# Seven half-size products instead of eight for the retention half of the merge, with the sums of tokens and weights on GpSimd

## The reference

```
y_mla = mla_branch(...) * silu(gate_mla)                 # 1024 x 1024
y_ret = retention_branch(q, k, v) * silu(gate_ret)       # 1024 x 2048, with a gain g_ret per column
merged = (sigmoid(merge_mla) * (y_mla @ w_proj_mla)      # weight 1024 x 1024
          + sigmoid(merge_ret) * (y_ret @ w_proj_ret))   # weight 2048 x 1024
x = x + gate * (merged @ w_out);  out = rmsnorm(x, g_final)
```

## Time and profile before

| | |
|---|---|
| runs | 1599.46, 1597.55, 1598.85 us; median 1598.85 |
| profiled execution | span 1596.8 us from the first to the last instruction; no time of its own around it is given, the median of the runs is 2.05 above the span |
| PE | busy 1560.5 us (98%), 7568 matmuls |
| DVE, ACT, POOL | 950.3 (60%), 615.3 (39%), 304.5 (19%) |
| DMA | 280.67 MB, mean 176 GB/s |

### The profile page before, as it was taken

The page is one execution under the profiler, slowest core; times in us unless marked ns, Lnnn a source line. Parts: engine busy times, 40 slices in busy tenths (PEclk is TensorE's granted clock), DMA queues, the critical chain, the costliest instruction groups (busy, mean ns, idle before and its releaser), DMA issues. The chain is left out here.

```text
span 1596.8 us, 20305 instructions
## 1 busy us (share of the span) xinstructions
PE 1560.5 (98%) x7568; PEld 1304.3 (82%) x7568; DVE 950.3 (60%) x1625; ACT 615.3 (39%) x1068; POOL 304.5 (19%) x270
## 2 busy tenths in 40 slices
PE   5999999999999999999999999999999999999998
PEld 4788888888888888798888888887688888888886
DVE  6884444444444457752576665767878775647544
ACT  7553333333333343442343333434544444213111
POOL 0032332232222200200000000025555530000000
PEclk9999999999999999999999999999999999999999
DMA  9332332332233334799264554448967767345332
GB/s 382 106 135 107 112 112 106 117 121 106 106 112 108 97 95 166 308 412 331 90 210 168 179 196 169 172 162 286 320 211 244 241 215 264 122 152 170 136 106 79
DMA packets 142977, 280.67 MB, mean 176 GB/s; under 512 B 11280, under 2 KB 84112, under 8 KB 134176
## 3 DMA queue, kind: packets, MB, share of 16 engines
q1 hardware_dynamic: 126160, 246.92, 44.6%
q10 hardware_dynamic: 12080, 15.60, 2.9%
q0 software_dynamic: 4640, 16.84, 2.7%
HBM read 183.65 MB, written 94.63 MB: 174 GB/s over the span
## 5 line engine op out<-in xcount | busy, mean ns | idle before, releaser
L1638 DVE TENSOR_TENSOR w_form<-w_pair,w_form 128x512 fp32r<-128x512 f32 x150 | 116.1, 775 | 125.1 <-ACT w_form L1260 123.3
L1260 ACT ACTIVATE w_form<-w_pair 128x512 fp32r<-128x512 f32 x150 | 95.0, 634 | 240.7 <-PE p_banks L2168 235.7
L1335 ACT ACTIVATE prob<-p_banks,neg_max 128x128 f32<-128x128 f32 (+3 forms) x64 | 47.6, 743 | 182.9 <-DVE neg_max L1765 182.9
L2165 PE MATMUL p_banks<-h_hi,w_form 128*128 128x512 f32 x300 | 116.7, 389 | 0.0
L2167 PE MATMUL p_banks<-h_lo,w_form 128*128 128x512 f32 x300 | 116.7, 389 | 0.0
L2168 PE MATMUL p_banks<-h_hi,w_form 128*128 128x512 f32 x300 | 116.7, 389 | 0.0
L539 ACT ACTIVATE w_hi<-w_raw 128x1024 fp32r<-128x1024 f32 (+3 forms) x63 | 53.3, 849 | 140.7 <-PE p_banks L2423 96.8
L2423 PE MATMUL p_banks<-y_hi,w_lo 128*128 128x512 f32 x256 | 99.6, 389 | 0.0
L2422 PE MATMUL p_banks<-y_lo,w_hi 128*128 128x512 f32 x256 | 99.6, 389 | 0.0
L2421 PE MATMUL p_banks<-y_hi,w_hi 128*128 128x512 f32 x256 | 99.6, 389 | 0.0
L1077 POOL DMA_DIRECT2D v_ret<-v_stage x32 | 17.6, 550 | 398.9 <-DVE v_stage L1742 398.7
(11 more groups left out here) (320 smaller groups left out, 4285.9 us busy)
## 6 DMA issues: line engine op xcount, KB each, us to landing
w_pair<-in_w_pairs SPq DMA_DIRECT2D x25, 1024.0 KB, 4.9
w_raw<-in_w_dense SPq DMA_DIRECT2D x39, 512.0 KB, 4.8
v_ret<-v_stage POOLq DMA_DIRECT2D x32, 512.0 KB, 3.6
v_chunk<-v_ret SPq DMA_DIRECT2D x32, 512.0 KB, 3.7
merge_t<-act_t SPq DMA_DIRECT2D x48, 256.0 KB, 3.5
act_t<-stage SPq DMA_DIRECT2D x40, 256.0 KB, 2.0
act_t<-stage_late SPq DMA_DIRECT2D x40, 256.0 KB, 2.0
ada<-in_w_ada SPq DMA_DIRECT2D x4, 2048.0 KB, 24.9
```

The source lines that it names most:

```text
L1260: self.nc.scalar.activation(self.form[f % FORM_SLOTS][:, 0, :], self.form_source(f), ACT.Copy).then_inc(self.form_hi, 1)
L1335: nc.scalar.activation(self.prob[:, g % 2, 0:width], p[:, 6:8, :].rearrange("p a n -> p (a n)")[:, 0:width], ACT.Exp, bias=self.neg_max[:, ...
L1638: nc.vector.tensor_tensor(self.form[f % FORM_SLOTS][:, 1, :], self.form_source(f), self.form[f % FORM_SLOTS][:, 0, :].bitcast(F32), ALU.su ...
L2165: self.nc.tensor.matmul(out, w_hi[:, cut], x_hi[:, q, :], start=fresh and q == 0, stop=False, skip_group_check=True)
```

## The change

The product of 1024 tokens x 2048 by 2048 x 1024 is taken as 2 x 2 blocks: tokens by even and odd chunk, inner dimension by even and odd head, columns by even and odd tile. Seven products of sums of blocks take the place of eight of blocks. One product is four units (`QUADS`), a unit is 8 x 3 matmuls with a weight tile of its own, so 28 units take the place of 32. The token operands: the blocks themselves for products 0, 2 and 4, and sums `t_sums` for 1, 3, 5 and 6, made on POOL from the chunks in the loop and stored to DRAM. The weight operands: blocks for 0, 2 and 6, sums made on POOL for 1, 3, 4 and 5 (`w_kept`, or in the raw place). Products 2 and 4 are accumulated onto the banks of 0 and 1; copies of 0 and 1 are taken by ACT. g_ret moves from the split of y_ret into the stored gates.

```
+RET_PRODUCTS = 7
...
+RAW_BLOCK = (A11, A21, A12, A11, A12, A11, A22)
+SECOND_BLOCK = {1: A22, 5: A21}
+SUMMED = (1, 3, 4, 5)
...
+GATED = (2, 4, 5, 6)
...
+GROUPS_SPLIT = ((0, 1), (2,), (3,), ())
+GATE_ROW_AT, GATE_ROW_UNIT = 4, 22
+OUT_SPLIT = {21: (0,), 25: (1, 2), 26: (3, 4), 27: (5, 6, 7)}
+OUT_ORDER = (1, 3, 5, 7, 0, 2, 4, 6)
...
@@ SP, retention loop, step n @@
             h, m = divmod(n, NT)
+            if n % 2 and n >= 3:
+                self.store_first_sums(sp, n - 2)
+                self.store_other_sum(sp, n - 2)
+            if n % 2 and h % 2:
+                self.load_first_half(sp, n)
+            if n % 2 == 0 and n and (n - 1) // NT % 2:
+                self.load_other_half(sp, n - 1)
+            if n == CHUNK_STEPS - 1:
+                for slot in (0, 2):
+                    sp.wait_ge(*self.yr_stored_by(24 + 4 + slot - 8))
+                for g in range(T_GROUPS):
+                    self.load_t_operand(sp, 0, g)
             sp.wait_ge(self.yr_done, n + 1)
...
+    def load_first_half(self, sp, k):
...
+        sp.wait_ge(self.t_sum_stored, HALF_FROM + 16 * (k // 2))
+        sp.dma_start(self.half_sum[0][:, :, :], self.chunk_of(self.d["t_sums"][0], k)).then_inc(self.half_loaded[0], 16)
...
+    def load_t_operand(self, sp, product, g):
+        if product < 2:
+            k = 4 * product + g
+            sp.wait_ge(*((self.set0_free, k + 1) if k < KD - 1 else (self.merge_summed, 2 * KD)))
+        else:
+            sp.wait_ge(self.ret_summed, QUADS * (product - 1))
...
@@ SP, merge @@
+        for u in range(1, RET_UNITS):
+            self.load_weight(sp, R_RET + u + RING + 1)
+            self.load_second(sp, u + RING + 1)
...
+            if quad == 1 and 1 <= product < RET_PRODUCTS - 1:
...
+                for g in range(T_GROUPS):
+                    self.load_t_operand(sp, product + 1, g)
...
@@ POOL, retention loop, step n, and after it @@
             self.rotate_chunk(pool, n)
+            if n >= 4 and n % 2 == 0:
+                self.first_sums(pool, n - 3)
+            elif n >= 5:
+                self.other_sum(pool, n - 4)
+        for k in (CHUNK_STEPS - 3, CHUNK_STEPS - 1):
+            self.first_sums(pool, k)
+            self.other_sum(pool, k)
+        self.gpsimd_output(pool)
...
+    def first_sums(self, pool, k):
...
+        if k // NT % 2 == 0:
+            nc.gpsimd.tensor_tensor(even, odd, even, ALU.subtract).then_inc(self.t_sums_done, 1)
+            return
...
+        nc.gpsimd.tensor_tensor(half, odd, half, ALU.subtract).then_inc(self.t_sums_done, 1)
+        pool.wait_ge(self.t_sums_done, before + 1)
+        nc.gpsimd.tensor_tensor(even, half, even, ALU.subtract).then_inc(self.t_sums_done, 1)
...
@@ POOL, gpsimd_output, for product in SUMMED, quad in range(QUADS) @@
+                if product == 1:
+                    ins = nc.gpsimd.tensor_tensor(kept, raw, second, ALU.add)
+                elif product == 5:
+                    ins = nc.gpsimd.tensor_tensor(raw, raw, second, ALU.subtract)
...
@@ ACT, pairs of the input projection, the retention gates @@
+            self.nc.scalar.activation(self.out_stage[out], source, ACT.Silu).then_inc(self.gate_scaled, 1)
...
+            ins = self.nc.scalar.activation(self.out_stage[out], self.out_stage[out], ACT.Copy,
+                                            scale=self.t["cols"][:, col:col + 1])
...
@@ ACT, merge @@
+        for g in range(T_GROUPS):
+            self.high_t(act, 0, g)
+        self.split_weight(act, R_RET + RING - 1)
+        for u in range(RET_UNITS):
+            product, quad = divmod(u, QUADS)
+            act.wait_ge(self.ret_summed, u + 1)
+            self.split_weight(act, R_RET + u + RING)
...
+            if product < RET_PRODUCTS - 1:
+                for g in GROUPS_SPLIT[quad]:
+                    self.high_t(act, product + 1, g)
...
+            if product >= 4:
+                self.high_merged(act, u)
+            for k in OUT_SPLIT.get(u, ()):
+                self.split_out_weight(act, k)
...
@@ DVE, end of the retention loop @@
+        for g in range(T_GROUPS):
+            self.low_t(dve, 0, g)
         for unit in range(units, 2 * KD):
             self.merge_unit(dve, unit)
...
@@ DVE, merge @@
+        for u in range(RET_UNITS):
+            product, quad = divmod(u, QUADS)
+            self.ret_outputs(dve, u)
+            self.lower_weight(dve, R_RET + u + RING)
+            if product < RET_PRODUCTS - 1:
+                for g in GROUPS_SPLIT[quad]:
+                    self.low_t(dve, product + 1, g)
+            if 0 <= u - GATE_ROW_AT < KD:
+                self.weigh_gate(dve, u - GATE_ROW_AT)
...
+            if product >= 4:
+                self.low_merged(dve, u)
+            for k in OUT_SPLIT.get(u, ()):
+                self.lower_out_weight(dve, k)
...
@@ DVE, ret_outputs(u) @@
+        if product == 2:
+            self.add_gated(dve, u, bank)
+        elif product == 3:
...
+            nc.vector.tensor_tensor(first, bank, first, ALU.add).then_inc(self.second_sums, 1)
+        elif product == 4:
...
+            nc.vector.tensor_tensor(bank, bank, first, ALU.add).then_inc(self.c_full, 1)
...
+            self.add_gated(dve, u, bank)
+        elif product == 5:
+            nc.vector.tensor_tensor(third, bank, first, ALU.add).then_inc(self.third_sums, 1)
+            nc.vector.tensor_tensor(fifth, third, fifth, ALU.add).then_inc(self.c_full, 1)
...
+            self.add_gated(dve, u, fifth)
+        elif product == 6:
+            nc.vector.tensor_tensor(third, third, bank, ALU.subtract).then_inc(self.c_full, 1)
...
+            self.add_gated(dve, u, third)
...
@@ PE, ret_products(u) @@
+        pe.wait_ge(self.w_lo_ready, R_RET + u + 1)
...
+        for k in range(KD):
+            g, part = divmod(k, 2)
+            if quad == 0 and part == 0:
+                pe.wait_ge(self.t_lo_ready, T_FROM + T_GROUPS * product + g + 1)
...
```

More of the change, by code:

```diff
@@ L475, in weight @@
             return a["w_v_up"][i], KKV * 256
+        if kind == "s":
+            product, quad = divmod(i, QUADS)
+            return a["w_ret"][4 * quad + RAW_BLOCK[product]], D
         base = dict(l=0, x=LAT_TILES, r=LAT_TILES + RAW, p=LAT_TILES + RAW + V_GROUPS * V_PARTS)
@@ L670, in units_after, with t_sums_before, other_sums, yr_stored_by @@
         return plan[min(step, len(plan) - 1)] // UNIT if step >= 0 else 0
+    def t_sums_before(self, k):
+        return sum(3 if n // NT % 2 else 1 for n in range(1, k, 2))
+    def other_sums(self, k):
+        return sum(n // NT % 2 for n in range(1, k, 2))
+    def yr_stored_by(self, n):
+        h, m = divmod(n, NT)
+        return self.yr_stored[h % 2][n % 4], YR_FROM + 16 * (2 * (h // 2) + m // 4 + 1)
+    def gated_unit(self, u):
+        product, quad = divmod(u, QUADS)
+        return QUADS * GATED.index(product) + quad if product in GATED else None
+    def ret_bank(self, u):
+        product, quad = divmod(u, QUADS)
+        return (ODD_BANKS if product in (1, 4, 6) else EVEN_BANKS)[quad]
+    def ret_block(self, tensor, gated):
+        product, quad = divmod(gated, QUADS)
+        tile, odd = 2 * quad + product // 2, (0, 1, 1, 0)[product]
+        return tensor(tile).rearrange("p (a e n) -> p a e n", e=2, n=P)[:, :, odd, :]
+    def t_source(self, product):
+        quads, sums = self.d["y_quads"], self.d["t_sums"]
+        return (quads[0, 0], sums[0], quads[1, 0], sums[1], quads[1, 1], sums[2], sums[3])[product]
+    def m_hi_at(self, k, n):
+        if k % 2 == 0:
+            return self.m_hi_even[:, k // 2, n * P:(n + 1) * P]
+        return self.m_hi_odd[n % 2][:, k // 2, n // 2 * P:(n // 2 + 1) * P]
     def states_before(self, n):
@@ L1425, in scalar_retention @@
             for k in SET0_SPLIT.get(n, ()):
-                self.split_set(act, 0, k)
-            for k in SET1_SPLIT.get(n, ()):
-                self.split_set(act, 1, k)
-            while units < self.set_units(n):
+                self.split_set(act, k)
+            while units < min(self.set_units(n), 2 * KD - 2):
                 if units % 2 and units > 1:
@@ L1811, in merge_unit @@
         nc = self.nc
-        z_set, part = divmod(unit, 2 * KD)
-        tile, half = divmod(part, 2)
+        tile, half = divmod(unit, 2)
         gate = self.merge_t[:, unit % 2, :]
@@ L1826, in merge_unit, with merge_bank @@
-        nc.vector.tensor_tensor(out, out, gate, ALU.add).then_inc(self.merge_added, 1)
-    def merge_bank(self, unit):
-        if unit < 2 * KD:
-            return 1 + unit % 2
-        tile, half = divmod(unit, 2)
-        return MERGE_BANKS[tile % 4][half]
+        nc.vector.scalar_tensor_tensor(out=out, in0=gate, scalar=1.0, in1=self.p[:, self.merge_bank(unit), :],
+                                       op0=ALU.add, op1=ALU.mult).then_inc(self.merge_added, 1)
+    def merge_bank(self, unit):
+        return 1 + unit % 2
@@ L2414, in tensor_retention @@
             self.fill_set(pe, end)
-    def merge_products(self, unit, k):
```

(15 more changed lines are left out.)

584 lines of the change are left out of this document (359 added, 225 removed).

## The result

The changed kernel is slower by 0.8%: 1611.51 us median (1610.54 to 1613.23, 4 runs) against 1599.15 (1597.55 to 1600.86, 4 runs), a ratio of 1.0079 with a 95% interval of 1.0065 to 1.0093. The span of the profiled execution went from 1596.8 to 1608.7 us, +11.9. I had forecast 1584.4, within 1577 to 1591. The profiled executions of e2 and e4 were 4 and 6 us faster than the medians of their kernels, that of e7 was 3 slower.

A forecast was written before the change was run, and what follows sets the result against it. TensorE, busy 98% of the span, was taken as the bound. Span 1596.8 - 21.8 + 4.7 + 1.7 + 0.9 = 1582.3, plus 2.05 from span to median, gave 1584.4 us; range 1577 to 1591.

The forecast's parts named there:

- The 96 matmuls, -21.8 us: Retention products on PE: 672 matmuls instead of 768, at 0.2267 us each, all on the path: -21.8 us.
- Product 3 is 12.7, so that a lag from product 2 is gone by product 4: 0: DVE's list in product 3 is 12.7 us, leaving room to recover a lag from product 2 (19.5): 0.
- DVE in products 4 to 6, +1.7 and +0.9: DVE's fuller list, stretched by POOL sums, delays operand 6: +1.7 us; SP's late load of it: +0.9 of 0 to 2.
- The average cost of a sum: DVE beside POOL's 128x1024 weight sums in the products: each sum costs DVE 1.05 us.
- a rate of 1.75: DVE subtractions wholly beside a POOL operation were taken to stretch, 1.21 us instead of 0.69.
- DVE becomes the bound: Rival for three products: DVE lists of 21.9 + 25.7 + 20 us, 7 to 9 us of stall, 1589 to 1591; chance 0.11.
- Entry, +4.7: Start of the first product: PE waits 4.0 us for operand 0, plus 0.7 for splits beside POOL's sums: +4.7 us.
- The clock, put at 0 in the sum and at +3.4 in a rival with a chance of 0.07: Rival: granted clock falls in the entry gap, 3.4 us of full-speed work lost, 1587.8; chance 0.07.
- Retention loop, cover of 2.4 us on the rotation: Retention loop: POOL's sums delay rotation, but 2.4 us of margin remains before ACT takes the chunk: 0.
- the landing of a store of sums: SP's wait in the retention loop for stores just issued, before loading the half sum: 3.2 us.
- the rival of a loop paced by POOL: Rival: late half sums delay rotation, ACT, DVE and PE; up to 36 us, 1620; chance slower 0.07, equal 0.04.
- (a) to (e): Moved g_ret, ACT's copies and splits, accumulation and bank reuse, the tail, output weight splits: all hidden, 0 each.

The follow-up runs named there:

- e2: Changed kernel with POOL's 32 token sums in the retention loop cut from 128 to 2 columns per part, transfers kept: 1612.12 us, ratio 1.0072.
- e4: Changed kernel with SP's operand loads for products 2 to 6 moved one turn earlier: 1610.98 us, ratio 1.0061.
- e7: Changed kernel with the three load orders of e3, e4 and e5 together (e3: operand 0 loaded and split earlier), sums on POOL: 1601.76 us, ratio 1.0015.
- e14: e9 without the transfers of token sums and with POOL's 32 token sums cut to 2 of 128 columns: 1581.72 us, ratio 0.9883.
- e5: Changed kernel with gate-factor loads ahead of gate-row weight loads, and gate-row loads one turn later: 1606.09 us, ratio 1.0038.
- e1: Changed kernel with POOL's 16 weight sums cut from 1024 to 8 columns, waits and loads kept: 1603.86 us, ratio 1.0020.
- e8: e7 with the 16 weight sums on VectorE instead of POOL, as in e6: 1594.48 us, ratio 0.9977.
- e11: Kernel before, with 12 idle 128x1024 sums added on POOL in the first half of its retention products: 1599.46 us against 1599.42, ratio 1.0002.
- e13: e9 without the 32 stores and 16 loads of token sums and their waits, POOL's sums kept: 1587.74 us, ratio 0.9927.
- e6: Changed kernel with the 16 weight sums made by VectorE instead of POOL, SP's order unchanged: 1613.09 us, ratio 1.0090.
- e9: e8 with all four parts of operand 0 split after the work on the last chunk: 1594.26 us, ratio 0.9968.
- e12: e9 with operand 1 and weights 3 and 4 loaded earlier, and output weight 0 split later: 1591.38 us, ratio 0.9949.
- e10: e9 with POOL's 32 token sums cut to 2 of 128 columns, transfers kept: 1591.07 us, ratio 0.9949.

## Why the prediction was wrong

- **The 96 matmuls, -21.8 us: right.** 7472 matmuls instead of 7568, at the same distance. In e14, where the loop is as long as before, the ratio is 0.9883, 18.7 us of the 21.8.
- **"Product 3 is 12.7, so that a lag from product 2 is gone by product 4: 0": the step that failed in the products.** I summed what DVE has to do, and not what it waits for in order. SP's queue held a ring (gate row, gate factors) that kept DVE 4.5 us, and each operand was issued only in the second turn of its product, behind DVE's own split, so that DVE stood 26 us for operands. Cost in product 3: 4.3 us of wait and 25 x 0.07 = 1.75 of clock; shown by e5 (5 to 7 us) and by the trace of e4. The prediction follows SP's queue entry by entry at the end of the loop, and in the products for operand 6 alone. All three orders mended give 10 us (e7).
- **DVE in products 4 to 6, +1.7 and +0.9: cause right, size wrong.** Measured 9.7 us, and 3.2 of clock. Late loads and sums made it together: leaving out the weight sums alone takes 9 us off the whole (e1), mending the loads alone 10 (e7), and mending the loads and moving the sums 17 (e8). The average cost of a sum was near mine (0.8 in e1, 1.16 in e11, against 1.05), but it doesn't spread: up to 2.2 us of it fall on one operation, and that can be the one for which PE waits. I read the 1.21 us of the earlier trace rows as a rate of 1.75 beside the POOL operation of 313.86. It is a wait for the one before it, which the rows leave out:

```profile
312.60 1.30 POOL L1023 TENSOR_TENSOR w_sum<-w_pair 128x512 f32<-128x512 f32 x1
```

  It ends at 313.90 and the subtraction 0.56 us later, at 314.46; POOL's next, begun in between, ends 1.13 us after that. The rival "DVE becomes the bound" (7 to 9 us of stall) was near in size for this part, and I gave it 0.11.
- **Entry, +4.7: right** (4.96 + 0.20, where I had 4.0 + 0.7), only later as a whole by what the loop had lost.
- **The clock, put at 0 in the sum and at +3.4 in a rival with a chance of 0.07: wrong.** It fell at the entry (22.4 x 0.15 = 3.4, of which the matmuls lost 4.8 x 0.48 = 2.3) and twice more, which I had not considered; 8.4 us altogether by the stretches, 7.1 by the matmuls. It comes on top of long waits and is not a case beside others. The Trainium skill (TensorE: Matmul & The Clock Gate, Part 1) says that idleness throttles the array; the trace agrees, with a clock of 0.50 to 0.57 behind the three longest waits and 0.77 to 0.80 us for the next matmul instead of 0.50.
- **Retention loop, cover of 2.4 us on the rotation: 0 was wrong, +5.8 in the trace.** The failed number is the landing of a store of sums: I took 3.2 us from the stores of the kernel before, and those of `t_sums<-y_ret_stage` took 5.8 in the median and 6.30 in the chain above, with 3.00 for the half sum instead of 3.5. That is 2.6 us more than I counted and over the margin of 2.4, and ACT waits in order for the rotated chunk as the rival of a loop paced by POOL has it. Its size (up to 36 us) was far too large: from the 20th chunk result to the 28th the loop takes 59.3 us as before, although chunks 25 and 27 have the same sums. By chunk, the distances between results grew by 1.1 to 1.6 us at chunks 6, 8, 15, 18 and 29; only the chain of 15 to 18 was followed. The DMA share rose from 0.75 to 0.85, and fell back to 0.75 without the transfers (e13).
- **(a) to (e) at nothing: right** as far as the trace shows: from 100 to 570 us PE is busy throughout as before, and every wait of PE inside the products names `t_lo` or `w_lo`, none ACT or a bank.
- **One error in common.** I summed the work of each engine and took the loads as given, so that waits in order (SP for DVE, DVE for SP's loads, ACT for POOL) came out at nothing. These costs don't all add up in the same way: the three orders of loads do (0.0067 alone in sum, 0.0064 together), but moving the weight sums to DVE gave nothing alone (e6) and 0.0038, 6 us, behind them (e8). All mends together, with the last orders of e9 and e12, gave 20 us.

## What to carry to other kernels

When a change halves the time between weights, write out each engine's list with what every entry waits for, SP's above all: a queue in which one load waits for a step of DVE and the next load feeds DVE is a ring. Judge a mend that gives an engine more work only when its loads come in time, as e6 (nothing) against e8 (6 us) shows. Where a new load waits for a new store in a queue, count the store's landing under the load that the change itself brings. A POOL offload was free only where the other engine's two-input operations have room (e11); where they are the fullest list, the sums were cheaper on DVE itself (e8 against e7).

## What the runs showed of the hardware

- A DVE operation with two SBUF inputs and a POOL sum take turns: 128x1024 takes 1.22 us alone and up to 3.44 when POOL's 2.40 us sum is just under way, and POOL's own goes from 2.39 to 3.05 and 3.17. Operations that read PSUM stay at 0.69. The Trainium skill says so (SBUF — State Buffer, "SBUF: two separate sides": the shared pair of ports is an exclusive lock and no split of bandwidth, and the second operation is blocked until the first is through); the trace agrees, with the ends 1.09 and 0.56 us behind POOL's in e11.
- The places of the operands decide it, not the operation: the gate-row step of e4 (`scalar_tensor_tensor`, two SBUF inputs) took 3.42 us instead of 1.28, the same operation with one input from PSUM in e11 kept its 0.69.
- The clock fell behind waits of 2.04 (e12), 2.39 (e1), 2.52 (e5) and of 3.6 us and more, and did not behind others of 2.18 (the changed kernel), 2.63 (e8), 2.67 (e9), 3.28 (e13) and 3.35 (e10). What a wait of 2 to 3.4 us costs can't be said from its length.
- A store of 256 KB from `y_ret_stage` landed after 3.2 us in the median in the kernel before and 2.8 in e13; with the transfers of token sums it is 4.3 for the chunk results and 5.8 for the sums (the changed kernel).
- Whether fewer and larger stores would spare the loop is open: no run changed the size of the transfers against their number.
